# One dense block's gate map by one-hot matmuls, and the indirect writes paced by three per up tile

## The reference, cut to what matters

```python
eidx = ...   # N x 128: 8 heads x 16 picks, each i1 * 128 + i2
gate = softmax(sc).reshape(N, 128)
a    = einsum('nd,ned->ne', x, u_emb[eidx])
coef = gelu(a) * gate
out  = einsum('ne,ned->nd', coef, v_emb[eidx])
```

## Time and profile before

| | |
|---|---|
| median of 3 runs | 1741.58 us (1740.88 to 1742.72) |
| profiled execution | 1741.91 us, its span 1740.1 us |
| granted TensorE clock | 0.997 of full speed |
| PE busy | 1703.1 us (98%) |
| PEld busy | 1405.0 us (81%) |
| DVE busy | 1109.5 us (64%) |
| ACT busy | 576.9 us (33%) |
| POOL busy | 916.6 us (53%) |
| DMA | 351.05 MB in 182675 packets |

### The profile page before, as it was taken

How to read it: one execution, slowest core, us unless ns; L and a number is a source line. 1 busy time by engine, 2 the same in 40 slices (tenths; PEclk the granted TensorE clock), 3 DMA queues, 4 the chain that set the end, 5 groups by cost and what they waited for, 6 DMA issues and landing times.

```text
span 1740.1 us, 23687 instructions
## 1 busy us (share of the span) xinstructions
PE 1703.1 (98%) x7926; PEld 1405.0 (81%) x7926; DVE 1109.5 (64%) x2997; ACT 576.9 (33%) x925; POOL 916.6 (53%) x828
## 2 busy tenths in 40 slices
PE   7999999999999999999999999999999999999997
PEld 6877877878888878888888888888888888888886
DVE  4259968544789864444444444444788888888886
ACT  4333225334322322222222222224333333333333
POOL 3644400002344007777777777771777777777710
PEclk9999999999999999999999999999999999999999
DMA  5322231115677645445547444444999999999991
GB/s 161 105 61 61 61 71 48 44 61 206 210 262 245 217 136 145 146 143 147 143 146 244 147 144 146 143 147 149 384 391 385 368 370 365 374 375 367 368 334 49
DMA packets 182675, 351.05 MB, mean 202 GB/s; under 512 B 35600, under 2 KB 118928, under 8 KB 182448
## 3 DMA queue, kind: packets, MB, share of 16 engines
q1 hardware_dynamic: 147776, 282.74, 49.0%
q0 software_dynamic: 34816, 67.41, 10.8%
HBM read 289.04 MB, written 61.02 MB: 201 GB/s over the span
## 4 chain that ended last, share of the span: by engine, by line
PE 63%; DVE 0%; issue 0%; DVEq 0%; ACT 0%
PE psum L399 21%; PE psum L398 21%; PE psum L400 21%; DVE mixed L2022 0%; DVE mixed L1999 0%; DVEq L1946 0%; DVE rstd_final L812 0%; DVE rstd_final L810 0%; DVE rstd_final L816 0%; DVE rstd_final L814 0%; DVE rstd_final L808 0%; ACT rstd_final L2133 0%; DVE rstd_final L2008 0%; DVE rstd_final L2006 0%
## 5 line engine op out<-in xcount | busy, mean ns | idle before, releaser
L2208 POOL DMA_INDIRECT gate_map<-gate_total,gate_at x384 | 403.6, 1051 | 205.3 <-DVE same_expert L1953 114.7
L398 PE MATMUL psum<-x_hi,ts_hi_u 128*128 128x512 f32 x1024 | 399.7, 390 | 4.0 <-PEq L1568 2.2
L400 PE MATMUL psum<-x_hi,ts_lo_u 128*128 128x512 f32 x1024 | 399.1, 390 | 0.0
L399 PE MATMUL psum<-x_lo,ts_hi_u 128*128 128x512 f32 x1024 | 399.1, 390 | 0.0
L1456 DVE TENSOR_TENSOR ts_lo_u<-ts_raw_u,ts_hi_u 128x1024 fp32r<-128x1024 f32 x116 | 142.3, 1226 | 341.3 <-ACT ts_hi_u L1451 338.6
L398 PE MATMUL psum<-v_hi,c_hi 128*128 128x512 f32 x768 | 298.8, 389 | 0.0
L399 PE MATMUL psum<-v_lo,c_hi 128*128 128x512 f32 x768 | 298.8, 389 | 0.0
L400 PE MATMUL psum<-v_hi,c_lo 128*128 128x512 f32 x768 | 298.8, 389 | 0.0
L1487 ACT ACTIVATE ut_out_u<-psum 128x512 f32<-128x512 f32 x128 | 76.5, 598 | 495.7 <-PE psum L400 495.7
L2113 ACT ACTIVATE v_hi<-v_raw 128x1024 fp32r<-128x1024 f32 x128 | 135.8, 1061 | 312.5 <-PE psum L400 312.5
L398 PEld LDWEIGHTS psum<-x_hi,ts_hi_u 128*128 128x128 f32 x1024 | 192.6, 188 | 44.8 <-issue 2.7
(11 more groups left out here) (242 smaller groups left out, 2321.4 us busy)
## 6 DMA issues: line engine op xcount, KB each, us to landing
ts_raw_u<-in_peer_u SPq DMA_DIRECT2D x128, 512.0 KB
v_raw<-in_peer_v SPq DMA_DIRECT2D x128, 512.0 KB, 6.0
gate_map<-zeros SPq DMA_DIRECT2D x32, 768.0 KB, 6.5
up_acts<-ut_out_u SPq DMA_DIRECT2D x128, 192.0 KB, 1.9
act_in<-up_acts SPq DMA_DIRECT2D x128, 192.0 KB, 6.3
gate_in<-gate_map SPq DMA_DIRECT2D x128, 192.0 KB, 6.7
raw_in<-in_w_in SPq DMA_DIRECT2D x56, 256.0 KB, 2.8
ts_raw_wq<-in_peer_wq SPq DMA_DIRECT2D x16, 512.0 KB, 6.4
```

The costliest lines, as they stand in the source:

```text
L398: nc.tensor.matmul(out, l_hi, r_hi, start=first, stop=False)
L399: nc.tensor.matmul(out, l_hi, r_lo, start=False, stop=False)
L400: return nc.tensor.matmul(out, l_lo, r_hi, start=False, stop=last)
L2208: nc.gpsimd.indirect_dma_start(gate_cells, bass.IndirectOffsetOnAxis(places["gate_at"][:, b, j:j + 1], 0), dn.total[:, b, j:j + 1], None). ...
```

## The change

The third dense block (frames 256 to 383) no longer goes through indirect writes. Its part of the gate map is computed. For a frame let i1, i2 and g be its 128 picks. The 128 x 128 map of gates by (i1, i2) is the product over picks of one-hot(i1) and g times one-hot(i2). PE transposes i1, i2 and g of the block once; DVE writes g as three bf16 parts that add up to it, and for every 16 frames builds `one1` (one-hot of i1), `one2` (of i2) and `val2` (one2 times each part) in bf16; PE multiplies per frame one1 by the three parts into PSUM; ACT copies the banks to `stage`; SP stores it 32 frames at a time, in four pieces.

- In `route` the key numbers of all blocks are kept (`keys`), the zeros cover two blocks (512 KB a store instead of 768 KB), and `addresses` is left out for the third block.
- In `experts` PE first transposes, then runs two up tiles, and then after every two further tiles one step of 16 frames (`rows`), eight steps, then the plain loop.
- 256 indirect writes are left, in bursts of three per finished up tile (`BURST`), four in flight instead of six. DVE's sums follow the same count.
- SP issues one piece of `stage` per up tile from tile 7 to tile 22.

```diff
+HOT_BLOCKS = 1
+WRITTEN_BLOCKS = DENSE_BLOCKS - HOT_BLOCKS
+WRITTEN = WRITTEN_BLOCKS * P
+HOT = HOT_BLOCKS * P
+GATE_STEP, BANKROWS, PARTS, CHUNK_FRAMES, PIECES = 16, 4, 3, 32, 4
-                sp.dma_start(gates_d[:, rows], zeros[:].unsqueeze(1).broadcast_to([P, ZERO_ROWS, DENSE])).then_inc(zeroed, 16)
+                sp.dma_start(gates_d[:, rows, 0:WRITTEN], zeros[:].unsqueeze(1).broadcast_to([P, ZERO_ROWS, WRITTEN])).then_inc(zeroed, 16)
-    PER_TILE = 4
-    IN_FLIGHT = 6
+    WRITES = WRITTEN_BLOCKS * SLOTS
+    BURST_TILES, BURST = 1, 3
+    IN_FLIGHT = 4
+    STEP = GATE_STEP
+    STEPS = HOT // STEP
+    inner = CHUNK_FRAMES // STEP
+    banks = STEP // BANKROWS
+    STORES = HOT // CHUNK_FRAMES * PIECES
+    FIRST_STORE = 2 * inner + 3
+    MAPPED_TILES = 2 + 2 * STEPS
+            def spread_pairs():
+                for x in range(2):
+                    nc.vector.tensor_copy(gm.twice[:, x], psum[:, x, 0:HOT].unsqueeze(2).broadcast_to([P, HOT, 2])
+                                          ).then_inc(spread, 1)
...
+            def one_hots(n):
...
+                nc.vector.tensor_tensor(pairs(gm.one2[:]), keys_b, token(gm.twice[:, 1], n), ALU.is_equal).then_inc(one2_done, 1)
+                if n >= 2:
+                    dve.wait_ge(mapped, (n - 1) * banks)
+                nc.vector.tensor_tensor(pairs(gm.one1[:, n % 2]), keys_b, token(gm.twice[:, 0], n),
+                                        ALU.is_equal).then_inc(one1_done, 1)
+            def gate_parts(n):
...
+                for x in range(PARTS):
+                    last = nc.vector.tensor_tensor(pairs(gm.val2[:, n % 2, x]), pairs(gm.one2[:]), token(gm.g_twice[:, x], n),
+                                                   ALU.mult)
+                last.then_inc(hot_done, 1)
             for n in range(TILES):
                 if n + 2 < TILES:
                     ut.split_lo(nc.vector, dve, n + (R + 2))
-                for m in range(n * PER_TILE, min((n + 1) * PER_TILE, DENSE_BLOCKS * SLOTS)):
+                if n < 2 * STEPS:
+                    if n % 2 == 0:
+                        one_hots(n // 2)
+                    else:
+                        gate_parts(n // 2)
+                for m in range(totals_by(n), totals_by(n + 1)):
                     total_gate(m, *place(m))
+            def rows(n, par, first):
+                pe.wait_ge(hot_done, n + 1)
+                for r in range(STEP):
+                    q, at = divmod(r, BANKROWS)
+                    if at == 0 and not first:
+                        pe.wait_ge(staged, n * banks - (banks - 1 - q))
+                    out = psum[:, q, at * P:(at + 1) * P]
+                    for x in range(PARTS):
+                        last = nc.tensor.matmul(out, gm.one1[:, par, r], gm.val2[:, par, x, r], start=x == 0,
+                                                stop=x == PARTS - 1)
+                    if at == BANKROWS - 1:
+                        last.then_inc(mapped, 1)
+            turn_picks()
+            for par in range(2):
+                ut.product(nc, pe, x_hi, x_lo, R + par, par, False)
+            for step in range(2):
+                for par in range(2):
+                    ut.product(nc, pe, x_hi, x_lo, R + 2 + 2 * step + par, par, False)
+                rows(step, step, step == 0)
+            with pe.Fori(1, STEPS // 2) as it:
...
+                    rows(it * 2 + step, step, False)
+            with pe.Fori(MAPPED_TILES // 2, TILES // 2) as it:
+            def copy_rows(n):
+                ch, at = n // inner, n % inner * STEP
+                if n % inner == 0 and ch >= 2:
+                    act.wait_ge(gates_stored[ch % 2], 16 * PIECES * (ch // 2))
+                for q in range(banks):
+                    act.wait_ge(mapped, n * banks + q + 1)
+                    nc.scalar.activation(
+                        gm.stage[:, ch % 2, :, at + q * BANKROWS:at + (q + 1) * BANKROWS].rearrange("p i n -> p n i"),
+                        psum[:, q, :].rearrange("p (n i) -> p n i", i=NKEYS), ACT.Copy).then_inc(staged, 1)
+            def store_gates(k):
+                ch, x = divmod(k, PIECES)
+                if x == 0:
+                    sp.wait_ge(staged, (ch + 1) * inner * banks)
+                keys_x = slice(x * piece, (x + 1) * piece)
+                frames_x = slice(WRITTEN + ch * CHUNK_FRAMES, WRITTEN + (ch + 1) * CHUNK_FRAMES)
+                sp.dma_start(gates_d[keys_x, :, frames_x].rearrange("i p n -> p i n"),
+                             gm.stage[:, ch % 2, keys_x]).then_inc(gates_stored[ch % 2], 16)
-                if m % PER_TILE == 0:
-                    pool.wait_ge(ut.product_done, R + m // PER_TILE)
+                if m % BURST == 0:
+                    pool.wait_ge(ut.product_done, R + m // BURST * BURST_TILES)
```

More of the change, by code:

```diff
@@ L1775, in addresses @@
             def addresses(b):
-                i1, i2 = (picked[:, b % 2, t].rearrange("p h k -> p (h k)") for t in range(2))
+                i1, i2 = (keys[:, b, t].rearrange("p h k -> p (h k)") for t in range(2))
                 if b >= DENSE_BLOCKS:
@@ L1864, in _, with __init__ @@
                         ut.split_lo(nc.gpsimd, pool, t)
+class GateTotals:
+    def __init__(self, c, sb):
+        self.total = sb("gate_total", [P, WRITTEN_BLOCKS, SLOTS], c=c)
+        self.same = sb("same_expert", [P, 2, SLOTS], c=c)
+class GateTiles:
+    def __init__(self, c, sb):
+        self.stage = sb("gate_stage", [P, 2, NKEYS, CHUNK_FRAMES], c=c)
+        self.iota_b = sb("iota_b", [P, NKEYS], BF16, c=c)
+        self.g_t = sb("g_turned", [P, HOT], c=c)
+        self.g_b = sb("g_part_b", [P, PARTS, HOT], BF16, c=c)
+        self.g_f = sb("g_part_f", [P, PARTS - 1, HOT], c=c)
+        self.rest = sb("g_rest", [P, HOT], c=c)
+        self.twice = sb("key_twice", [P, 2, HOT, 2], BF16, c=c)
+        self.g_twice = sb("g_twice", [P, PARTS, HOT, 2], BF16, c=c)
+        self.one1 = sb("one1", [P, 2, GATE_STEP, NKEYS], BF16, c=c)
+        self.one2 = sb("one2", [P, GATE_STEP, NKEYS], BF16, c=c)
+        self.val2 = sb("val2", [P, 2, PARTS, GATE_STEP, NKEYS], BF16, c=c)
 class DownTiles:
@@ L1900, in experts @@
     FIRST_ROW = 10
-    PER_TILE = 4
-    assert PER_TILE * TILES >= DENSE_BLOCKS * SLOTS
-    IN_FLIGHT = 6
+    WRITES = WRITTEN_BLOCKS * SLOTS
+    BURST_TILES, BURST = 1, 3
+    assert (TILES - 6) // BURST_TILES * BURST >= WRITES
+    IN_FLIGHT = 4
     OUTS = 2 * DENSE_BLOCKS
     EARLY = RING
-    ndense = NB - DENSE_BLOCKS
-    assert ndense == 1
+    STEP = GATE_STEP
+    STEPS = HOT // STEP
+    PAIRS = NKEYS // 2
+    inner = CHUNK_FRAMES // STEP
+    banks = STEP // BANKROWS
+    piece = NKEYS // PIECES
+    STORES = HOT // CHUNK_FRAMES * PIECES
+    FIRST_STORE = 2 * inner + 3
+    MAPPED_TILES = 2 + 2 * STEPS
+    ndense = NB - DENSE_BLOCKS
+    assert ndense == 1 and 2 * inner == PIECES and STEPS % 2 == 0
+    FIRST_LOAD = max(TILES // 2, FIRST_STORE + STORES)
+    turned = sem("picks_turned")
+    g_split = sem("g_split")
+    spread = sem("twice_done")
+    one2_done = sem("one2_done")
+    one1_done = sem("one1_done")
+    hot_done = sem("one_hots_done")
+    mapped = sem("rows_mapped")
+    staged = sem("staged")
+    gates_stored = [sem(f"gates_stored{i}") for i in range(2)]
     totalled = sem("gates_totalled")
@@ new lines, in split_gates @@
+            def split_gates():
+                nc.vector.tensor_copy(gm.iota_b[:], iota[:])
+                nc.vector.tensor_copy(gm.g_t[:], psum[:, 2, 0:HOT]).then_inc(g_split, 1)
+                dve.wait_ge(g_split, 1)
+                nc.vector.tensor_copy(gm.g_b[:, 0], gm.g_t[:]).then_inc(g_split, 1)
+                dve.wait_ge(g_split, 2)
+                nc.vector.tensor_copy(gm.g_f[:, 0], gm.g_b[:, 0]).then_inc(g_split, 1)
+                dve.wait_ge(g_split, 3)
+                nc.vector.tensor_tensor(gm.rest[:], gm.g_t[:], gm.g_f[:, 0], ALU.subtract).then_inc(g_split, 1)
+                dve.wait_ge(g_split, 4)
+                nc.vector.tensor_copy(gm.g_b[:, 1], gm.rest[:]).then_inc(g_split, 1)
+                dve.wait_ge(g_split, 5)
+                nc.vector.tensor_copy(gm.g_f[:, 1], gm.g_b[:, 1]).then_inc(g_split, 1)
+                dve.wait_ge(g_split, 6)
+                nc.vector.tensor_tensor(gm.g_b[:, 2], gm.rest[:], gm.g_f[:, 1], ALU.subtract).then_inc(g_split, 1)
@@ new lines, in pairs, with token @@
+            def pairs(tile):
+                return tile.rearrange("p n (q t) -> p n q t", t=2)
+            def token(tile, n):
+                return tile[:, n * STEP:(n + 1) * STEP].unsqueeze(2).broadcast_to([P, STEP, PAIRS, 2])
+            def one_hots(n):
+                if n:
+                    dve.wait_ge(hot_done, n)
+                else:
+                    dve.wait_ge(spread, 2 + PARTS)
+                keys_b = gm.iota_b[:].rearrange("p (q t) -> p q t", t=2).unsqueeze(1).broadcast_to([P, STEP, PAIRS, 2])
```

(30 more changed lines are left out.)

54 lines of the change are left out of this document (33 added, 21 removed).

## The result

The changed kernel takes 1765.05 us (median of 4 runs, 1764.67 to 1767.21), the kernel before 1741.55 us in the same runs: ratio 1.0137, 95% interval 1.0119 to 1.0154. It is 23.5 us slower. The profiled execution took 1765.20 us, its span is 1763.3 us, 23.2 more than before.

The account below looks back on a forecast made before the run. PE was taken to bound the kernel: one-hot matmuls 25.6 us plus transposes 0.35, all else 0, sum 26.0; 1741.91 + 26.0 = 1767.9, less 0.33 gives 1767.6 us, range 1761 to 1790.

Parts of the forecast that it names:

- PE sets the end: 640 to 1190 us: PE busy 549.26 of 550.00 us, so added PE work costs fully and removed writes give nothing.
- The price of a pair: One-hot steps on PE: each bf16 weight load and matmul of 128 columns costs 66.7 ns, 384 of them 25.6 us.
- 14 ns per matmul that doesn't depend on the columns: PE matmuls: fixed part left after 53 ns per 128 columns, from 226.7 ns at 512 and 174 at 384 columns.
- the same line: PE matmul price as columns plus a fixed part, 53 + 14 = 67 ns at 128 columns, said to fit every product matmul.
- The lower bound: One-hot steps on PE: a quarter of the 512-column price, 56.7 ns per matmul, 21.8 us in all.
- The upper bound: One-hot steps on PE: priced as float32 matmuls of the same shape, 116 ns each, 44.5 us in all.
- rival of the weight load: One-hot steps on PE: a bf16 load takes as long as float32, 384 x 116 ns = 44.5 us, 1786 us; chance 16%.
- a bf16 load is half as long: One-hot steps on PE: bf16 weight load taken as 56 ns against float32's 112, hidden under 53 ns of columns or nearly.
- The waits at zero: Steps in experts: PE gets no new waits for DVE's one-hots, low splits or ACT's copies, 0 us.
- the double price that I allowed for: ACT's four bank copies per step: priced at 0.60 us each like a gelu; twice the time per copy still fits.
- The stores: 16 map stores on DMA: 17 ns a descriptor, just full, 0 us; rival of stalls, 1801 us at 30 ns, chance 12%.
- The clock: PE after the barrier, 642 to 645 us: low-clock loss of 8 x 0.2 us stays, value 0, bounds -1.6 and +1.6 us.

Follow-up runs that it names:

- e1: Changed kernel without the map's one-hot part (no transposes, products, matmuls, copies, stores), the 256 writes in bursts kept: 1742.33 us against 1742.29, ratio 1.0001.
- e3: Changed kernel with two of the three bf16 parts multiplied on PE, 256 matmuls instead of 384, DVE's work unchanged: 1757.07 us, ratio 1.0083.
- e5: Changed kernel with weights loaded once per four frames, 96 bf16 matmuls of 512 columns instead of 384 of 128: one run of 1766.55 us.
- e4: Changed kernel with float32 one-hots and the gate in one float32 part, 128 float32 matmuls instead of 384 bf16 ones: 1770.68 us, ratio 1.0164.
- e2: Changed kernel without the 16 stores of the staged map and the waits for them: 1763.20 us, ratio 1.0120.
- e6: Changed kernel with each store of the staged map cut in two, runs of 64 bytes instead of 128, 8192 descriptors a piece: 1793.03 us, ratio 1.0292.
- e10: Kernel before with what follows the routing stage's last up tile (gelu, high split, load, store) moved behind the barrier: 1739.30 us, ratio 0.9983.
- e7: Kernel before with 14 idle PE transposes behind the routing stage's last up tile, ahead of the barrier: ratio 1.0021 (0.9982 to 1.0059).
- e12: Changed kernel with what follows the routing stage's last up tile moved behind the barrier: 1762.31 us, ratio 1.0116.

## Why the prediction was right

The forecast was 1767.6 us, the result 1765.05. Point by point:

- *PE sets the end, all of its new time counts, nothing comes back.* Shown. e1 has 128 writes less and takes the time of before; e3 takes 7.1 us off PE's starts for 128 matmuls.
- *The price of a pair, 66.7 ns.* The mis-sized term: it measured 55.6 ns, so 21.3 us instead of 25.6. The step that failed is "14 ns per matmul that doesn't depend on the columns", read off fp32r rows and carried over to bf16. e5 shows that it doesn't carry over. Nor do all products fit the same line, which the prediction gives as its reason. It overlooked 48 matmuls in the kernel before, of fp32r and 128 columns, each with new weights:

```profile
407.53 0.27 PE L399 MATMUL psum<-x_lo,ts_hi_wq 128*128 128x128 f32 x1
...
412.67 0.28 PE L400 MATMUL psum<-x_hi,ts_lo_wq 128*128 128x128 f32 x1
```

  From the one to the other are 46 starts, 111.7 ns each and not 67; their loads are 0.11 us apart, too, as at L1031. So for four-byte operands the load sets the pace at 128 columns, and the line had no row where it was used. What kept the bf16 price low is what the prediction assumed without a row: the shorter load. That a line used beyond its reach still gave 67 for 55.6 is in part luck. The Trainium skill has the right figure in "TensorE: Matmul & The Clock Gate", section "Wait — 56ns, not 53.3ns?": the columns at 2.4 GHz plus about 2.5 ns. The trace agrees, 55.6 and 216 ns; the 81 ns that the same page gives in "Back-to-back issue gap" didn't hold.
- *The lower bound.* 56.7 ns, a quarter of an fp32r matmul, was no bound at all: the measured price is 1 ns below it, for the same reason.
- *The upper bound and the rival of the weight load.* The assumption "a bf16 load is half as long" fits the recorded durations (98 ns against 191 or 192); the pace of bf16 loads alone, which must be 55.6 ns or less, no run shows. But 116 ns is not the price of a float32 matmul: it is that of one of its two instructions. Had I counted the group against the code, x128 for 64 matmuls, the upper bound would have been 232 ns (e4 measured 224).
- *What the sum lacked.* 0.9 us behind the steps; 0.3 us for the transposes against 0.35. With the 4.3 us of the pair this leaves 0.7 us of differences ahead of and behind PE's work and between runs.
- *The waits at zero.* Right: PE has no new one. But ACT's copies take 0.99 us each, four in 3.97 us, not the 0.60 of a gelu, and only the double price that I allowed for covers them. They write with a stride of 128 bytes; whether this is why, no run shows.
- *The stores.* On the line between the packets of the earlier trace rows I had 17 ns a descriptor and a queue that is just full. The changed kernel's SP queue, 680 to 800 us:

```profile
q1 hardware_dynamic: 73421, 22.05, 89.2%
```

  Less e2's row for the same window, 65,500 packets take 48.9% of 16 engines' 120 us, 939 us of engine time: 14.3 ns each, where the line had 17 and the expectation of e6 16.6. With this a store takes 3.7 us of all engines, and the queue is near to full but not full. SP itself is held, too: the issue of the load behind a store takes 3.5 to 5.3 us instead of 0.45. The lead of the loads covers it. e6 shows the other side: twice the descriptors, of half the bytes, 28 us. With its 13.5 tiles at e2's price of 440 packets and 97.8 ns, its descriptors of 64 bytes come to 13.7 ns, an estimate: the number of the runs counts, and hardly their length.
- *The clock.* The value 0 was right for the two profiled executions: from 641 to 646 us the granted clock is 0.66 before and after. e2 is the lower bound come true, 1.6 us, and by the traces it is half of what e10 saves.

## What to carry to other kernels

When the bound engine is full, work moved onto it costs its full price, and work taken off an engine with slack gives nothing; find out which is which before sizing either. Take the price of a matmul from rows of its own operand type and number of columns, and count a group's rows against the code before dividing by them. When many short runs are stored, compare descriptors times some 14 ns with the time they have: here 4096 per tile were hidden and 8192 cost 28 us.

## What the runs showed of the hardware

- Pairs of load and matmul at 2.4 GHz: bf16 55.6 ns (128 columns) and 216 ns (512); fp32r 226.7 ns (512) and 111.7 ns (128); float32 224 ns (128 columns, two instructions).
- A store's descriptor costs 14.3 ns of one DMA engine at 128 bytes (the changed kernel against e2) and about 13.7 ns at 64 (e6).
- POOL's indirect write takes 0.96 us, but twice that while DVE compares or multiplies two bf16 tensors of 2048 elements. The changed kernel, by time; DVE's two comparisons run from 662.24 to 664.60 us:

```profile
663.46 1.96 POOL L2392 DMA_INDIRECT gate_map<-gate_total,gate_at  x1 [0.30 <-issue]
665.73 0.96 POOL L2392 DMA_INDIRECT gate_map<-gate_total,gate_at  x1 [0.30 <-DVE same_expert L2012]
```

  The Trainium skill, "Advanced Engine Details and Errata", section "GPSIMD Details", says that POOL shares a read and a write interface with DVE and conflicts with instructions that have two inputs in SBUF. The trace agrees: the bf16 instructions have two such inputs, and so has the low split of u, beside which the writes of the kernel before take up to 1.36 us. No experiment took the inputs one by one.
- After 1.9 to 2.2 us without a matmul, at the barrier, the granted clock fell to 0.50 for some 3 us in the kernel before, in the changed one and in e1 and e3 to e6, and not at all in e2. After 0.3 to 1.6 us (e7 to e12) it didn't fall there. But at 414 us, where every kernel is idle for 0.68 us, it fell in e1 and e5 and stayed up in the other twelve traces. So the length of the idle time alone doesn't decide; what else does stays open.
